# Expert blocks on one core: rows gathered and scattered per block, first block of each expert fixed, output and routing in the same stage

## The reference

```python
x = layer_norm(alpha * x + gate_1 * (merged @ w_out))          # 1024 x 1024
u = modulate(x, shift, scale)
g = argmax(u @ rt_group_w + b)                                  # 4 groups
top-2 of the 8 experts of that group, weights = softmax(top) * group_prob
# 2048 assignments, sorted by expert, in blocks of 128 rows of one expert
hid = silu(xb @ w_gate[e]) * (xb @ w_up[e])                     # 1024 -> 512
y   = hid @ w_down[e]                                           # 512 -> 1024
x = layer_norm(alpha * x + gate_2 * sum_r weight_r * y_r)
```

## Time and profile before

| | us |
|---|---|
| median of 3 runs | 3189.16 |
| runs | 3187.28 to 3192.15 |
| profiled execution, span from first to last instruction | 3182.9 |
| busy PE / DVE / ACT / POOL in the span | 2769.4 / 1631.1 / 996.2 / 279.9 |

### The profile page before, as it was taken

How to read it: one execution, slowest core, us unless ns; L and a number is a source line. 1 busy time by engine, 2 the same in 40 slices (tenths; PEclk the granted TensorE clock), 3 DMA queues, 4 the chain that set the end, 5 groups by cost and what they waited for, 6 DMA issues and landing times. The chain is left out here.

```text
span 3182.9 us, 33378 instructions
## 1 busy us (share of the span) xinstructions
PE 2769.4 (87%) x12400; PEld 2050.8 (64%) x12400; DVE 1631.1 (51%) x1517; ACT 996.2 (31%) x1104; POOL 279.9 (9%) x236
## 2 busy tenths in 40 slices
PE   7889898989999599999894999998918999999973
PEld 4443773335888577878773778784417888888861
DVE  4634336272332256343178262424627888888866
ACT  2302230001332133320000010001007888888860
POOL 1200000000000221000141300000010000000001
PEclk9889999999999788999996999998958999999996
DMA  6432454221232421211110111113149999999945
GB/s 213 132 126 112 166 205 135 89 86 60 67 108 84 135 78 52 71 53 51 40 51 14 47 34 47 43 30 121 50 189 366 371 375 374 371 371 371 373 183 224
DMA packets 92001, 482.89 MB, mean 152 GB/s; under 512 B 10836, under 2 KB 20324, under 8 KB 76745
## 3 DMA queue, kind: packets, MB, share of 16 engines
q1 hardware_dynamic: 71688, 382.41, 33.5%
q0 software_dynamic: 20224, 99.25, 8.3%
HBM read 424.01 MB, written 82.78 MB: 159 GB/s over the span
## 5 line engine op out<-in xcount | busy, mean ns | idle before, releaser
L337 PE MATMUL ps<-uT_upper_rest,ring_rest 128*128 128x512 f32 x1360 | 541.3, 398 | 0.0
L337 PEld LDWEIGHTS ps<-uT_upper_rest,ring_rest 128*128 128x128 f32 x1360 | 259.0, 190 | 66.1
L337 PE MATMUL ps<-uT_upper_rest,cs_upper 128*128 128x512 f32 x320 | 130.2, 407 | 55.0 <-DVE cs_val L1971 46.8
L2443 PE MATMUL ps<-ring_rest,uT_rest 128*128 128x256 f32 (+1 forms) x416 | 135.2, 325 | 26.2 <-DVE uT_upper_rest L2520 26.2
L2445 PE MATMUL ps<-ex_u_raw_rest,uT_rest 128*128 128x256 f32 x560 | 156.6, 280 | 0.0
L2443 PE MATMUL ps<-ex_upper,uT_rest 128*128 128x256 f32 (+1 forms) x424 | 136.3, 322 | 21.0 <-DVE uT_upper_rest L2520 21.0
L337 PE MATMUL ps<-uT_upper_rest,xbc_upper 128*128 128x512 f32 x336 | 136.0, 405 | 6.1 <-DVE ring_rest L727 6.1
L1744 PE MATMUL ps<-sb_merged,ring 128*128 x256 | 114.5, 610 | 26.0 <-DVE sb_merged L1819 26.0
L2444 PE MATMUL ps<-ex_upper,uT_rest 128*128 128x256 f32 (+1 forms) x424 | 134.3, 317 | 0.0
L337 PE MATMUL ps<-uT_rest,xbc_upper 128*128 128x512 f32 x336 | 134.2, 399 | 0.0
L2444 PE MATMUL ps<-ring_rest,uT_rest 128*128 128x256 f32 (+1 forms) x416 | 133.3, 320 | 0.0
(11 more groups left out here) (437 smaller groups left out, 6305.6 us busy)
## 6 DMA issues: line engine op xcount, KB each, us to landing
sb_spare<-in_ex_g SPq DMA_DIRECT2D x35, 2048.0 KB
ex_u_raw<-in_ex_u SPq DMA_DIRECT2D x35, 2048.0 KB
sb_merged<-in_ex_d SPq DMA_DIRECT2D x35, 2048.0 KB, 10.3
ring<-in_w_mod SPq DMA_DIRECT2D x48, 512.0 KB, 4.5
sb_uT<-moe SPq DMA_DIRECT2D x35, 512.0 KB, 12.0
moe<-sb_uT POOLq DMA_DIRECT2D x35, 512.0 KB, 8.0
ring<-in_w_gate SPq DMA_DIRECT2D x32, 512.0 KB, 3.6
ring<-in_dft SPq DMA_DIRECT2D x24, 512.0 KB, 3.6
```

The lines of the kernel that those rows point to most:

```text
L337: last = self.nc.tensor.matmul(out, weight, x[:, k, lo:hi], start=(k == 0 and n == 0), stop=(k == kt - 1 and n == 2))
L2443: nc.tensor.matmul(out, left_up, w_up, start=first, stop=False)
```

## The change

The stages output, route and experts become one stage and one program for each engine. `moe` and its zero fill go; `u_tok` (1024 rows, u in HBM) and `y_rows` (2048 rows, one for each assignment, first choices first) come. Block slots: 32 fixed ones, the first 128 rows of each expert, and up to 16 extra ones for what is over 128. From `place` DVE builds two one-hot arrays and PE turns them into a list of 128 assignment ids for each of the 48 slots; a slot without a row gets an id out of bounds.

```diff
+EXTRA = (2 * T - 1) // P + 1
+SLOTS = EXPERTS + EXTRA
...
-            @block.gpsimd
-            def _(pool):
-                blank = a["moe"].rearrange("(n p r) d -> n p (r d)", p=P, r=4)
...
-                    pool.dma_start(blank[m], a["zeros"]).then_inc(k.blank, 16)
...
+        def fixed_blocks(eng, body):
+            for b in range(2):
+                body(b, b, 0)
+            with eng.Fori(1, EXPERTS // 2) as j:
+                for b in range(2):
+                    body(j * 2 + b, b, j)
...
+        def extra_blocks(eng, body):
+            n = extra_count(eng)
+            with eng.Fori(0, EXTRA // 2) as j:
+                for b in range(2):
+                    with eng.If(j * 2 + b < n):
+                        body(j * 2 + (EXPERTS + b), b, j + EXPERTS // 2)
+            return n
```

SP asks for the first two experts' weights while the output tiles are made, and needs no value for the fixed blocks:

```diff
+                    if t in (1, 3):
+                        sp.dma_start(raw[0][:, t // 2, :], item(a["ex_g"], t // 2)).then_inc(w_in[0][t // 2], 16)
+                sp.wait_ge(mix_mm, TT)
+                for b in range(2):
+                    for m, name in ((1, "ex_u"), (2, "ex_d")):
+                        sp.dma_start(raw[m][:, b, :], item(a[name], b)).then_inc(w_in[m][b], 16)
...
-                    sp.dma_start(x[:, 1 - b, :], item(rows, after)).then_inc(x_in[1 - b], 16)
```

POOL stores each tile of u, and gathers and scatters for each block (its 35 turns are written out, those of extra blocks behind an `If`):

```diff
+                    pool.wait_ge(u_ready, t + 1)
+                    pool.dma_start(a["u_tok"][t * P:(t + 1) * P, :], u[:, t, :]).then_inc(u_out, 16)
...
+                def gather(i):
+                    if i:
+                        pool.wait_ge(x_mm, i + 1)
+                    pool.indirect_dma_start(out=x[:, i % 2, :], out_offset=None, in_=a["u_tok"],
+                                            in_offset=bass.IndirectOffsetOnAxis(gather_at[:, i:i + 1], 0),
+                                            bounds_check=T - 1, oob_is_err=False).then_inc(x_in[i % 2], 16)
+                def scatter(i):
+                    pool.wait_ge(y_ready, i + 2)
+                    pool.indirect_dma_start(out=a["y_rows"],
+                                            out_offset=bass.IndirectOffsetOnAxis(scatter_at[:, i:i + 1], 0),
+                                            in_=y, in_offset=None,
+                                            bounds_check=2 * T - 1, oob_is_err=False).then_inc(y_out, 16)
+                gather(0)
+                gather(1)
+                for i in range(EXPERTS):
+                    gather(i + 2)
+                    scatter(i)
...
-                pool.wait_ge(k.blank, 16 * k.blank_parts)
-                for t in range(TT):
-                    for r in range(2):
-                        pool.indirect_dma_start(out=a["moe"], out_offset=bass.IndirectOffsetOnAxis(dest[:, r, t:t + 1], 0),
-                                                in_=k.uT[:, t, :], in_offset=None).then_inc(sent, 16)
-                pool.wait_ge(sent, 2 * TT * 16)
-                pool.dma_start(x[:, 0, :], a["moe"][0:P, :]).then_inc(x_first, 16)
```

PE gets 16 matmuls for the ids. ACT rounds four chunks of the first expert around its two Exps, and loads Silu's table by hand; its y copy waits for the scatter before:

```diff
+                for n in range(2 * TT):
+                    mm = nc.tensor.matmul(ps[:, 7, 0:SLOTS], in_block[:, n, :], of_block[:, n, :],
+                                          start=(n == 0), stop=(n == 2 * TT - 1))
...
+                cast_first(0)
+                cast_first(1)
+                act.wait_ge(g_exp_in, 1)
+                nc.scalar.activation(g_exp, cand_g, ACT.Exp).then_inc(g_exp_ready, 1)
+                act.wait_ge(d_ready, 1)
+                nc.scalar.activation(which, which, ACT.Exp).then_inc(d_exp_ready, 1)
+                nc.scalar.preload_act_table(ACT.Silu)
+                for b in range(2):
+                    act.wait_ge(h_out[b], 16 * TT // 2)
+                cast_first(2)
+                cast_first(3)
...
-                    act.wait_ge(y_free, i + 1)
+                    if not isinstance(i, int):
+                        act.wait_ge(y_out, i * 16 - 16)
```

DVE's routing is the same up to the counts. The softmax weights and the owners of the extra blocks move behind the ids; `place` gets four 256-wide steps in place of one, and there are new steps for the ids:

```diff
+                do(ts(cand, rank, float(P), float(P), ALU.is_ge, ALU.mult))
+                do(tt(cand, cand, to_tiles(shift, E), ALU.mult))
+                do(tt(place, cand, rank, ALU.add))
+                do(stt(out=place, in0=to_tiles(iota[:, 0:E], E), scalar=float(P), in1=place, op0=ALU.mult, op1=ALU.add))
...
+                do(tt(of_block[:, :, :], index(SLOTS), hot_at(at_f[:, 1, :], SLOTS), ALU.is_equal))
+                tt(of_block[:, :, :], of_block[:, :, :].bitcast(F32), hot_at(k.const("assign"), SLOTS),
+                   ALU.mult).then_inc(hot_ready, 1)
+                tt(in_block[:, :, :], index(P), hot_at(at_f[:, 0, :], P), ALU.is_equal).then_inc(hot_ready, 1)
+                v.wait_ge(ids_mm, 1)
...
+                nc.vector.tensor_copy(gather_at[:, :], gather_f[:, :]).then_inc(ids_ready, 1)
+                nc.vector.tensor_copy(scatter_at[:, :], ids_f[:, :]).then_inc(ids_ready, 1)
...
+                for m in range(2):
+                    rest_chunk(0, 0, m)
```

In the combine stage, SP loads y as plain runs, ahead of h1 in each tile:

```diff
+                def load(t):
+                    for r in range(2):
+                        sp.dma_start(y[r][:, t, :], a["y_rows"][r * T + t * P:r * T + (t + 1) * P, :]).then_inc(y_in[t], 16)
+                    sp.dma_start(h1[:, t, :], a["h1"][t]).then_inc(h_in[t], 16)
...
-                        pool.indirect_dma_start(out=y[r][:, t, :], out_offset=None, in_=a["moe"],
-                                                in_offset=bass.IndirectOffsetOnAxis(dest[:, r, t:t + 1], 0)
-                                                ).then_inc(y_in[t], 16)
```

More of the change, by code:

```diff
@@ L2253, in _ @@
                                  start=False, stop=True)
-                nc.tensor.matmul(ps[:, 1, 0:E], k.ones[:, :], every[:, :], start=True, stop=True).then_inc(rank_mm, 1)
-            @block.scalar
-            def _(act):
-                act.wait_ge(g_ready, 1)
-                nc.scalar.activation(g_exp[:, :, :], cand_g[:, :, :], ACT.Exp).then_inc(g_exp_ready, 1)
-                act.wait_ge(d_ready, 1)
-                nc.scalar.activation(which[:, :], which[:, :], ACT.Exp).then_inc(d_exp_ready, 1)
@@ new lines, in _, with do, to_tiles, wide @@
+                take_logits(TT - 2)
+                take_logits(TT - 1)
+                v.wait_ge(logit_ready, TT)
+                def do(ins):
+                    ch.step(ins)
+                    ch.wait()
+                def to_tiles(row, width):
+                    return row.unsqueeze(1).broadcast_to([P, TT, width])
+                def wide(w, width):
+                    return w.unsqueeze(2).broadcast_to([P, TT, width])
+                tt, ts, stt = nc.vector.tensor_tensor, nc.vector.tensor_scalar, nc.vector.scalar_tensor_tensor
@@ new lines, in _ @@
+                do(reduce(group, cand_g, AX.X, ALU.min))
+                do(tt(miss_g, to_tiles(iota[:, 0:G], G), wide(group, G), ALU.not_equal))
+                do(ts(miss_g, miss_g, -BIG, None, ALU.mult))
+                for t in range(TT):
+                    ch.step(tt(own[:, t, :].rearrange("p (g e) -> p g e", g=G),
+                               logits[:, t, G:G + E].rearrange("p (g e) -> p g e", g=G),
+                               miss_g[:, t, :].unsqueeze(2).broadcast_to([P, G, MOE_EPG]), ALU.add))
@@ new lines, in _ @@
+                do(tt(chosen, hot[:, 0, :, :], hot[:, 1, :, :], ALU.add))
+                do(nc.vector.memset(before[:, 0, :], 0.0))
+                for t in range(1, TT):
+                    do(tt(before[:, t, :], before[:, t - 1, :], chosen[:, t - 1, :], ALU.add))
+                tt(every, before[:, TT - 1, :], chosen[:, TT - 1, :], ALU.add).then_inc(rank_in, 1)
+                tt(which, best[:, 1, :], best[:, 0, :], ALU.subtract).then_inc(d_ready, 1)
+                v.wait_ge(rank_mm, 1)
@@ new lines, in _ @@
+                do(stt(out=place, in0=to_tiles(iota[:, 0:E], E), scalar=float(P), in1=place, op0=ALU.mult, op1=ALU.add))
+                for r in range(2):
+                    do(tt(cand, hot[:, r, :, :], place, ALU.mult))
+                    do(reduce(dest[:, r, :], cand, AX.X, ALU.add))
+                do(nc.vector.tensor_copy(place_i[:, 0, :], dest.rearrange("p r t -> p (r t)")))
+                ch.step(ts(place_i[:, 1, :], place_i[:, 0, :], 7, None, ALU.logical_shift_right))
+                ch.wait()
```

504 lines of the change are left out of this document (247 added, 257 removed).

## The result

The changed kernel takes 3081.12 us (median of 4 runs, 3075.05 to 3086.44) against 3188.22 (4 runs, 3183.95 to 3192.15) for the kernel before on the same chip: ratio 0.9667, 95% interval 0.9649 to 0.9684, some 107 us less. A second group of five runs gave 3080.58 and the ratio 0.9689 (0.9667 to 0.9710).

A forecast was written before the change was run, and what follows sets the result against it. Bound: the block chain through PE, hid cast, table load, x_up, chunk cast and DVE's rest, 19.72 us. Sum 38.8 + 43.9 - 1.5 + 1 + 7.7 = 90 off 3182.9, plus 6.3: 3099; range 3085 to 3144.

The forecast's parts named there:

- launch and end: Whole run: the median's 6.3 us above the profiled span, put down to these and added to 3092.9, giving 3099.
- the price of a table load: ACT between last hid cast and x_up: removing the load moves the next block up by 1.29 us.
- Block: Expert loop: 19.72 us falls to 18.43, saving 43.9 over 34 blocks, less 1.5 for entering a second loop.
- What is next: Expert loop: with the load gone, PE's own 18.28 us of work stands just under 18.43 of chain.
- Combine: Combine stage: plain y loads let PE start 5 us after the expert stage instead of 12.7, 7.7 less.
- Start: Last logits to first gate product: barriers, scatters and read back go, weights come early; 38.8 us less.
- Last y copy to first diagonal: End of expert stage: POOL skips 12 unrolled conditions in place of 13 in a loop, 0 us.
- Less traffic: Expert blocks: only real rows move, 6.77 MB for 7.34; makes room for the faster block, gains nothing itself.
- Table loads stay: Rival: expert loop keeps its table loads, block stays 19.72 us, time 3143; chance 0.10.
- DMA takes over: Rival: skipped rows move too, blocks need 19.0 to 19.7 us, time 3118 to 3143; chance 0.11.
- DVE held up by POOL: Rival: POOL's index reads delay DVE's first rest, block 19.4 us, 33 lost, time 3132; chance 0.06.
- Gather late: Rival: PE waits for x before its turn if landing exceeds 16.3 us; at 19.5, time 3214; chance 0.04.

The follow-up runs named there:

- load in the chain: Changed kernel with one table load per block put back between the last hid cast and the x_up copy: 3127.41 us, ratio 0.9825 to the kernel before.
- scatters and late weights: Changed kernel with the sixteen token-row scatters put back before the blocks and the first experts' weights requested only beside them: ratio 0.9796 to the kernel before.
- combine: Changed kernel with the combine stage's sixteen y loads issued again as indirect gathers by POOL: ratio 0.9704 to the kernel before.
- second run of the changed one: Changed kernel measured again unaltered, as baseline of a later group: 3080.58 us, ratio 0.9689; 768.5 us from last logits to the end.
- the kernel before, preloaded: Kernel before with one Silu table preload added ahead of its block loop: 3133.13 us, ratio 0.9842.
- all rows: Changed kernel with the rows that no token fills gathered and scattered too: ratio 0.9683 to the kernel before.

## Why the prediction was right, and where it was wrong

**Direction and mechanism: right.** Gains were forecast at three places for three reasons, and all three were found there: the table loads on the block's chain, the scatters at the start, the gathers in the combine. Put back one at a time, they cost 45.4 (load in the chain), 38.9 (scatters and late weights) and 8.1 (combine) in R, 92.4 of the 95.9 that part the kernel before from the second run of the changed one. The rest is small: the load at the last y copy gave 1.3.

**The steps that failed are two terms of the sum, both in size:** the 6.3 us added for launch and end, of which the runs show 1.6 to 2.6, and the price of a table load, 1.29, of which they show 1.42 on the chain.

**The time: too high by 18 us.** Seven come from the last step, "launch and end explain" the 6.3 between span and median. They don't: in each execution of the changed kernel's first group the time is 1.6 to 2.6 above the span, and in all 34 later ones of the kernel before 1.9 to 2.0. The profiled execution of the kernel before was quicker than its group, some 3184.9 by that distance beside a median of 3189.16, and the one of the changed kernel was not (3081.9 beside a median of 3081.12). The other eleven are 101.0 for 90:
- *Block*, 42.4 forecast, 47.5 measured. The load was priced at 1.29, start to start of the load and x_up; on the chain it is worth 1.42, since the overlap with the instruction ahead comes back too. 34 times 0.13 is 4.4. By the same sum the chain would be 18.30 and not 18.43, and 18.29 was measured. The passage to the extra blocks costs 0.9 (19.26 for the 18.38 of that turn) and the last block 0.3, so the 1.5 taken for it was about right. The drain of 1.38 that the Trainium skill adds for a switch to another set (ScalarE: Activation LUTs, What ACT_TABLE_LOAD costs) isn't there: the load put back, of a table that is loaded already, made the block 1.38 longer in all, of which 1.28 is the load itself. In the kernel before, with two loads in each block, taking both out shortened the block by 1.33 (19.72 to 18.39).
- *What is next*: PE at 18.28 just under the chain. It is just under it, at 18.22.
- *Combine*, 7.7 and 9.1. What was forecast is PE's start, 5 behind the first diagonal for 12.7, and it was 5.2. The rest lies between PE's start and the first combined tile, 5.2 for 6.7, and it doesn't repeat: in other executions of the same text C is up to 11.8.
- *Start*, 38.8 and 40.0. The sum was right for a reason that it only half named: it counted the scatters and the read back, but that the weights beside them slowed the scatters' landing, from 5.0 us alone to 15.5 in the experiment, wasn't seen.
- *Last y copy to first diagonal*, 0 forecast, 1.1 lost. The conditions weren't what lost it, they take 2.5 less than before; POOL's drain takes 2.9 more and had no term.
- *Ahead of the stage*, 0 forecast, 3.9 measured, within the 12 us by which that mark moves. The medians of the groups differ by 102 to 107 where R explains 95 to 97; whether some 5 us of real gain lie ahead of the last stage stays open. The zeros are not it.
- *Less traffic*, 0 forecast, and 0 it is, but not because it "makes room": the kernel before, preloaded, moved all its bytes at 398 GB/s in blocks of 18.39.

**The range** began at 3085, and the time fell 4 below it. It held no term for the spread between executions, some 10 us from lowest to highest here, nor one for the 6.3, and the terms' errors nearly all lay on one side. With 1.6 to 2.6 in place of the 6.3 it would have begun at 3080 to 3081, where the measured time lies.

**The rivals.** *Table loads stay*: no load in the loop. The reading of the loop with four Sigmoids in the earlier trace rows held, and one preload took them out of the old loop as well. *DMA takes over*: the rows skipped move nothing, and moving them costs nothing. *DVE held up by POOL*: DVE's rests take 2.28 as before; it is the other way round, see the last section. *Gather late*: gathers land in 8.7 (8 forecast), 11.3 with all rows, far from 16.3.

Of the marks named: x_lo 18.32 apart for 18.4; no loads; DMA share 0.96 at 370 GB/s; first gate product 39.7 behind the logits for 41.

## What to carry to other kernels

Find the chain first, then price an instruction on it by the distance that its neighbours would have without it, not by its duration: here 1.28 was worth 1.42 in one place and nothing in another. An engine that is busy 400 us of 400 need not be the limit (here it fell 0.07 us a block short of being it); leaving out some of its work, or moving a step of the chain, tells. And compare two kernels from a mark that both pass, not by their spans, when what lies ahead of it moves by more than the effect.

## What the runs showed of the hardware that was not expected

POOL's indirect scatters take 2.61 us each in the mean, its gathers 1.04. Groups by line of the changed kernel (busy, mean ns | idle before), and a scatter in the timeline with DVE's rest beside it:

```profile
L2250 POOL DMA_INDIRECT y_rows<-sb_uT,ex_scatter_at x35 | 91.5, 2614 | 295.5 <-ACT sb_uT L2430 285.3 <-issue 10.2
```

```profile
2688.19 4.49 DVE L2463 TENSOR_TENSOR ex_u_raw_rest<-ex_u_raw,ex_upper 128x2048 fp32r<-128x2048 f32 x2
2690.88 2.68 POOL L2250 DMA_INDIRECT y_rows<-sb_uT,ex_scatter_at  x1 [8.75 <-ACT sb_uT L2430]
```

The last scatter, with DVE idle, takes 1.01 (3000.33 above). It isn't a matter of scatter or gather: the one gather that falls beside a weight rest takes 2.41, and those beside hid_lo or x_lo, which have one of their inputs in PSUM, take 1.0.

```profile
2963.41 4.48 DVE L2463 TENSOR_TENSOR ex_u_raw_rest<-ex_u_raw,ring_rest 128x2048 fp32r<-128x2048 f32 x2
2964.16 2.41 POOL L2243 DMA_INDIRECT sb_uT<-u_tok,ex_gather_at  x1 [13.61 <-issue]
```

Each long one ends about 0.9 us behind the end of the rest that was running when it started. So the two do meet, as the Trainium skill says of a DVE instruction with two SBUF inputs (SBUF — State Buffer, Who interferes with whom), but it is POOL, which starts second each time, that is held up and not DVE, and POOL has time.

The DMA engines moved some 400 GB/s through the expert stage with no wait for them in the blocks, though the earlier trace rows has a share of 0.96 at 372 already: the share is close to full well before the rate is.
